# Strassen's seven products for five pairs of output tiles of a hybrid decoder layer, one Trainium2 core

## The chip, the core and the metric

The kernel runs on one core of one Trainium2 chip. The metric is the device time of one execution in microseconds (us): the median of several executions, lower is better. The core has TensorE (PE, the matrix unit), VectorE (DVE), ScalarE (ACT), GpSimd (POOL), and SyncE (SP), which here only issues DMA transfers. The engines run side by side, each through its own list of instructions in order, and wait for one another with semaphores.

## The reference

One layer of a decoder for 512 prompt tokens and 8 sample tokens, all in float32, d_model 2048.

```python
h = rms_norm(xp, norm_g[l])
u, gp, q, k, v, ga = split_proj(h, w_in[l])          # 2048 -> 6144
pm, pbuf = pool_mix(u, zero_buf, 0, pool_w[l], pool_scale[l])
a = dilated_attn_prompt(q, k, v, slopes)
xp = xp + merge_out(pm, gp, a, ga, w_out[l], xp.dtype)
...
y_prompt = rms_norm(xp, final_norm_g)
...
def merge_out(pm, gp, a, ga, w_out, dtype):
    mix = jnp.concatenate([pm * jax.nn.silu(gp), a * jax.nn.silu(ga)], axis=-1)
    return jnp.einsum('btm,md->btd', mix, w_out)     # 2048 x 2048: the part that changes
```

The same is done for the 8 sample tokens, which attend to a cache.

## The kernel before

**Layout.** Tokens lie along the free dimension: 520 columns (512 prompt, 8 sample), of which a matmul takes about half (260, or 256 and 264), since a PSUM bank holds 512 values. Features lie on the 128 partitions, 16 blocks of 128. Every float32 product is made of three matmuls: both operands are split into a high part, which is the value rounded to the matmul's input type, and the rest, the low part, and high times high, high times low and low times high are added up in PSUM. The moving side is in `mov_hi` and `mov_lo`. The weights come by DMA into `w_raw`, ACT writes the high part (`split_hi`, L884) and DVE the low part (`split_lo`, L1224).

**Stages.** The program is a list of steps. Steps 0 to 143 are the input projection in 144 chunks, 18 to a pair of heads, with the attention and the pooling branch of the previous and the present pair of heads woven in. Steps n = 0 to 47 after them (n counts from IN_CHUNKS = 144) are the output projection: 16 tiles of 128 output features, three chunks each (6, 5 and 5 of the 16 blocks of the contraction: 36, 30 and 30 matmuls). Tiles 0, 1 and 2 run interleaved (n = 0 to 8), since parts of the moving side still come in then. Tiles 3 to 13 follow one after another from n = 9, 96 matmuls each. Tiles 14 and 15 are done apart, first for the last 256 prompt tokens and the 8 samples (`half_chunk`, L719, n = 42 to 47), then for the first 256 tokens with the roles of weights and tokens exchanged (`row_chunk`, L730).

**What happens around a tile.** Each engine goes through the same list of steps. SP loads the chunk of step n + 3 (`load_chunk`, L452 to L459; it first waits until the slot of `w_raw` has been split). ACT and DVE split the chunk of step n + 2. One step after a tile's last chunk DVE transposes its 520 columns out of PSUM in blocks of 32 (`turn_out`, L1667 to L1669). Two steps after it SP sends the blocks to DRAM with 8 transfers (`send_tile`, L522 and L524), four steps after it SP reads them back in natural order with 2 transfers (`load_rows`, L530 and L532), five steps after it DVE adds the residual (`add_res`, L1682 and L1684), and ACT squares and sums the five row groups for the final norm (`y_square`, L1079). Six steps after it DVE multiplies with the final gain (`scale_y`, L1693 and L1694). SP loads the residual of a tile with 3 transfers (`load_res`, L537 to L540); those of tiles 0 to 2 are issued at n = 7, behind waits for the moving side to be split and for the k and v stores. `half_evict(14)` (L1068), at n = 45 on ACT, takes tile 14 out of PSUM, `turn_half(14)` (L737) on PE waits for it, and PE goes on with tile 15 behind it. After the last tiles a chain of small DVE and ACT instructions makes the norm and SP stores the rows.

**Queues.** No instruction of an engine passes another. SP's list holds the weight loads, `send_tile`, `load_rows` and `load_res` in the order of the steps. POOL has nothing to compute after the first 20 us of the program but issues some stores.

## Time and profile before

| what | value |
|---|---|
| median of 3 executions | 844.7 us (842.57 to 845.32) |
| span of the profiled execution, first to last instruction | 840.8 us |
| PE busy | 830.5 us, 99% of the span, 6825 matmuls |
| DVE busy | 566.8 us, 67% |
| ACT busy | 375.4 us, 45% |
| POOL busy | 60.8 us, 7% |
| DMA, mean over the span | 156 GB/s |
| output projection, tiles 3 to 13 on PE | 681.96 to 808.70 us |

The profiled execution has no total time of its own beside its span; the median of the three timed executions is 3.9 us above it, for what lies before the first and behind the last instruction. In the views below a name in the program such as `arena` stands for many buffers that share it. An instruction's duration reaches from its start to its result, so that consecutive instructions of one engine overlap in part: a matmul of 260 columns lasts about 280 ns, but a new one starts every 120 ns.

### The profile page before, as it was taken

What the parts mean: (1) busy time and instruction counts of PE and PEld (TensorE: products, weight loads), DVE (VectorE), ACT (ScalarE), POOL (GpSimd) and SP (SyncE); (2) the same over time, 40 slices, a digit from 0 to 9 for tenths busy, and PEclk for the clock granted to TensorE, in tenths of its full rate; (3) what the DMA queues carried; (4) which work ended last, traced back from release to release, by engine and by line L of the source; (5) the groups of instructions that cost most, each with busy time, mean ns of one, the idle gap of its engine ahead of it and who ended that gap; (6) DMA issues with size and microseconds to landing.
All of it is one profiled execution on the core that took longest, in us unless ns stands there. A gap on an engine that the chain in (4) does not pass through costs nothing.

```text
span 840.8 us, 17357 instructions
## 1 busy us (share of the span) xinstructions
PE 830.5 (99%) x6825; PEld 825.0 (98%) x6825; DVE 566.8 (67%) x1240; ACT 375.4 (45%) x821; POOL 60.8 (7%) x116
## 2 busy tenths in 40 slices
PE   9999999999999999999999999999999999999996
PEld 8999999999999999999999999999999999999995
DVE  5646784796579667957884797579888535444456
ACT  5745435523553454245535533553455325333444
POOL 2001100201010001001100201010000100000000
PEclk9999999999999999999999999999999999999998
DMA  8576247536643753575356437643768566766665
GB/s 291 149 174 166 84 126 181 134 96 171 165 115 87 192 148 82 150 183 145 92 134 170 128 94 201 166 111 93 179 184 279 162 168 172 179 178 176 177 169 204
DMA packets 274601, 131.51 MB, mean 156 GB/s; under 512 B 69056, under 2 KB 268160, under 8 KB 274496
## 3 DMA queue, kind: packets, MB, share of 16 engines
q1 hardware_dynamic: 269912, 122.90, 54.9%
q0 software_dynamic: 4608, 7.50, 2.7%
q8 instruction: 54, 0.88, 0.5%
q14 instruction: 27, 0.22, 0.1%
HBM read 110.32 MB, written 18.92 MB: 154 GB/s over the span
## 4 chain that ended last, share of the span: by engine, by line
PE 89%; DVE 4%; SPq 2%; DMA 2%; ACT 1%; issue 1%; DVEq 0%; ACTq 0%
PE pj L693 77%; PE ps_t L737 2%; PE ps_o L781 1%; PE ps_s L752 1%; PE ps_s L750 1%; PE ps_o L779 1%; DMA out<-arena 1%; SPq L486 1%; PE ps_o L693 1%; PE ps_s L798 1%; PE ps_t L798 1%; PE ps_s L693 1%; PE ps_s L631 1%; DVE w_lo L1224 1%; DVE arena L1339 1%
## 5 line engine op out<-in xcount | busy, mean ns | idle before, releaser
L693 PE MATMUL pj<-mov_hi,w_hi 128*128 128x260 f32 (+2 forms) x1952 | 399.2, 286 | 0.3 <-DVE mov_lo L1245 0.3
L693 PE MATMUL pj<-mov_hi,w_lo 128*128 128x260 f32 (+2 forms) x1952 | 392.9, 283 | 0.0
L693 PE MATMUL pj<-mov_lo,w_hi 128*128 128x260 f32 (+2 forms) x1952 | 392.4, 283 | 0.0
L693 PEld LDWEIGHTS pj<-mov_hi,w_hi 128*128 128x128 f32 x1952 | 300.9, 188 | 0.9 <-issue 0.7
L693 PEld LDWEIGHTS pj<-mov_hi,w_lo 128*128 128x128 f32 x1952 | 301.0, 188 | 0.0
L693 PEld LDWEIGHTS pj<-mov_lo,w_hi 128*128 128x128 f32 x1952 | 300.9, 188 | 0.0
L884 ACT ACTIVATE w_hi<-w_raw 128x640 fp32r<-128x640 f32 (+1 forms) x187 | 144.5, 773 | 261.4 <-PE pj L693 234.9
L1224 DVE TENSOR_TENSOR w_lo<-w_raw,w_hi 128x640 fp32r<-128x640 f32 (+1 forms) x187 | 161.7, 865 | 143.0 <-ACT w_hi L884 142.7
L944 ACT ACTIVATE pt_hi<-ps_t 128x128 fp32r<-128x128 f32 (+1 forms) x64 | 26.2, 436 | 80.3 <-PE ps_t L737 78.3
L1315 DVE TENSOR_TENSOR pt_lo<-ps_t,pt_hi 128x128 fp32r<-128x128 f32 (+1 forms) x64 | 29.7, 484 | 45.6 <-ACT pt_hi L944 45.4
L1262 DVE SCALAR_TENSOR_TENSOR arena<-pj,rstd_bc 128x260 f32<-128x260 f32 (+2 forms) x104 | 36.8, 398 | 12.1 <-PE pj L693 10.4
L928 ACT ACTIVATE arena<-arena,stat 128x128 f32<-128x128 f32 (+1 forms) x64 | 35.8, 559 | 19.3 <-DVE stat L1301 18.7
L1301 DVE CUSTOM_DVE_ANT_0 arena<-ps_s,arena 128x128 f32<-128x128 f32 (+1 forms) x64 | 29.7, 481 | 16.9 <-PE ps_s L752 16.9
L936 ACT ACTIVATE arena<-arena,stat 128x128 f32<-128x128 f32 (+1 forms) x64 | 34.2, 557 | 15.3 <-DVE stat L1309 15.2
L1079 ACT ACTIVATE arena<-arena 128x128 f32<-128x128 f32 (+1 forms) x70 | 21.7, 311 | 28.3 <-DVE arena L1684 26.6
L1375 DVE TENSOR_TENSOR arena<-arena 128x128 f32<-128x128 f32 (+3 forms) x48 | 28.8, 601 | 1.6
L1339 DVE TENSOR_TENSOR arena<-arena 128x1024 f32<-128x1024 f32 (+2 forms) x24 | 26.0, 1083 | 1.6 <-DMA out<-arena 1.6
L1342 DVE TENSOR_REDUCE arena<-arena 128x16 f32<-128x1024 f32 (+2 forms) x24 | 26.1, 1086 | 0.8
L737 PE MATMUL ps_t<-tab,arena 128*128 128x128 f32 x162 | 25.7, 273 | 0.6 <-DVE pt_lo L1315 0.5
L1366 DVE TENSOR_TENSOR arena<-arena 128x1024 f32<-128x1024 f32 (+2 forms) x24 | 25.4, 1086 | 0.2
L1183 POOL DMA_DIRECT2D out<-arena x32 | 16.3, 510 | 105.0 <-DVE arena L1614 105.0
L737 PEld LDWEIGHTS ps_t<-tab,arena 128*128 128x128 f32 x162 | 19.5, 141 | 3.1 <-ACT arena L936 0.7
(245 smaller groups left out, 810.5 us busy)
## 6 DMA issues: line engine op xcount, KB each, us to landing
w_raw<-in_w_in SPq DMA_DIRECT2D x96, 320.0 KB, 3.5
w_raw<-in_w_in SPq DMA_DIRECT2D x48, 384.0 KB, 3.7
arena<-in_cache_k_win SPq DMA_DIRECT2D x16, 384.0 KB
arena<-in_cache_v_win SPq DMA_DIRECT2D x16, 384.0 KB
w_raw<-in_w_out SPq DMA_DIRECT2D x16, 384.0 KB, 3.7
w_raw<-in_w_out SPq DMA_DIRECT2D x16, 320.0 KB, 3.9
arena<-in_cache_k_win SPq DMA_DIRECT2D x8, 512.0 KB
arena<-in_cache_v_win SPq DMA_DIRECT2D x8, 512.0 KB
```

The costliest lines, as they stand in the source:

```text
L693: mm = pe.matmul(dst[h][:, 0:own.stop - own.start], w, m[:, k, own], start=(k == 0 and i == 0), stop=(c == 2 and k == KT - 1 and i == 2))
L737: return pe.transpose(dst, src, ident[0:n, 0:n])
L884: act.activation(w_at(n)[0][:, 0:hi - lo, :], w_raw[:, n % SLOTS, 0:hi - lo, :], ACT.Copy).then_inc(w_hi_done, 1)
L928: act.activation(pb_, pb_, ACT.Exp, scale=-1.0, bias=nmax[:, i:i + 1], accum_out=den[:, i:i + 1]).then_inc(exped, 1)
L936: a = act.activation(pb_, pb_, ACT.Copy, scale=rden[:, i:i + 1])
L944: a = act.activation(pt_hi[:, 0:i + 1, P * i:P * i + P], ps_t[:, at:at + P * (i + 1)].rearrange("p (j x) -> p j x", j=i + 1), ACT.Copy)
L1224: dve.tensor_tensor(to_lo[:, 0:hi - lo, :], w_raw[:, n % SLOTS, 0:hi - lo, :], to_hi[:, 0:hi - lo, :].bitcast(F32), ALU.subtract).then_inc ...
L1262: o = dve.scalar_tensor_tensor(out=dst, in0=pj[a][h][:, c0:c1], scalar=scale, in1=rstd_bc[:, HT * h + c0:HT * h + c1], op0=ALU.mult, op1=A ...
L1301: dve.tensor_tensor_reduce(out=pbuf[r % 2][:, at:at + n], in0=ps_s[:, at:at + n], in1=nbias[:, SEQ - n:SEQ], scale=1.0, scalar=3e38, op0=A ...
L1315: o = dve.tensor_tensor(pt_lo[blk], ps_t[:, at:at + P * (i + 1)].rearrange("p (j x) -> p j x", j=i + 1), pt_hi[blk].bitcast(F32), ALU.subt ...
L1339: dve.tensor_tensor(ks, ks, q_rep.unsqueeze(1).to_broadcast([P, hi - lo, P]), ALU.mult).then_inc(kq_prod, 1)
L1375: o = dve.tensor_tensor(out, vv[:, P * to:P * (to + n)], vv[:, P * other:P * (other + n)], ALU.add)
```

## The change

Output tiles 3 to 12 are done as five pairs (m1, m2). The contraction of a pair is cut: blocks 0 to 3 and 4 to 7 of the moving side form a two by two problem with the two tiles and the two halves of the columns (260 each). It is done with seven block products in place of eight (Strassen's scheme in Winograd's form); blocks 8 to 15 are multiplied as before. A block product is 12 matmuls (4 blocks of the contraction, three matmuls each).

- **Weights.** A pair has eleven units of 4 blocks (512 columns): `w11`, `w12`, `w22`, the sums `s1` to `s4`, and `std1x`, `std1y`, `std2x`, `std2y` for the plain half. Each is split by ACT and DVE into a ring of six places (`unit_hi_of`, `unit_lo_of`). The four sums are made by POOL (`weight_sum`), in the order s1, s2, s3, s4, from the raw weights of 4 blocks each (`raw_a`, `raw_b`, `raw_c`, `raw_e`). s2 waits until s1 is split, since both use `raw_s`, and s4 until s2 is.
- **Moving side.** Once, at n = 2 to 7, DVE adds high and low parts of blocks 0 to 7 back together (`whole_x`, 2 instructions of 2080 columns), makes four combinations (`form_sums`, 4 of 1040 columns), and ACT and DVE split them (4 each of 1040 columns).
- **PSUM.** A pair uses four banks, a to d. The running sum in bank a is copied out by ACT at four points (`snapshot`), and PE waits for the copy before it goes on in that bank. `meet` (DVE) adds the snapshots to the banks, `turn_both` transposes a tile.
- **Steps.** A pair takes six steps k = 0 to 5 with 36, 24, 24, 36, 24 and 36 matmuls (`duo_step`), 180 in place of 192; in the first pair step k = 0 has only 12, since nothing is left over from a pair before. Pair 0 begins at n = 9, and tile 13 follows at n = 39 to 41 as a tile alone. The first tile of a pair is done in k = 4 and the second in k = 1 of the next pair.
- **SP.** A pair has 14 weight transfers where two tiles had 8. The residuals of tiles 0 to 2 are loaded at n = 8 and wait for the first two forms to be split (`m_split` 8).

Some semaphores are shared by two uses (`x_in`, `ms_done`, `sd_done`, `rs_done`), and several buffers lie over one another (`parts`); that is left out of the diff. In it, `...` marks what is left out.

```diff
+WOVEN = 3
+DUOS = 5
+SEVEN = WOVEN * 3
+DUO_STEPS = 6
+AFTER = SEVEN + DUOS * DUO_STEPS
+SOLO = WOVEN + 2 * DUOS
...
+RING = 6
+UNITS_OF = ("w11", "s1", "s2", "std1x", "std1y", "s3", "w12", "s4", "w22", "std2x")
+RING_SEQ = tuple((p - (u == "std2y"), u) for p in range(DUOS) for u in (
+    UNITS_OF[:1] + ("std2y",) * (p > 0) + UNITS_OF[1:])) + ((DUOS - 1, "std2y"),)
+RING_N = {pu: n for n, pu in enumerate(RING_SEQ)}
...
+        def chunk_at(step):
+            if IN_CHUNKS + SEVEN <= step < IN_CHUNKS + AFTER:
+                return None
+            return step if step < IN_CHUNKS + SEVEN else step - DUOS * DUO_STEPS
+        def duo_at(step):
+            n = step - IN_CHUNKS - SEVEN
+            return divmod(n, DUO_STEPS) if 0 <= n < DUOS * DUO_STEPS + 3 else None
+        def split_ahead(step):
+            n = step - IN_CHUNKS
+            if n <= SEVEN - 3 or n >= AFTER + 1:
+                return (chunk_at(step + 2),) if n < OUT_CHUNKS - 2 else ()
+            return {AFTER - 1: (chunk_at(step + 1),),
+                    AFTER: (chunk_at(step + 1), chunk_at(step + 2))}.get(n, ())
+        def units_ahead(step):
+            n = step - IN_CHUNKS - SEVEN
+            p, k = divmod(n, DUO_STEPS)
+            at = {0: ("s2", "std1x"), 1: ("std1y", "s3"), 2: ("w12", "s4", "w22"), 3: ("std2x",),
+                  4: ("std2y", "w11"), 5: ("s1",)}[k]
+            own = [(p + (u in ("w11", "s1")), u) for u in at]
+            own.sort(key=lambda pu: RING_N.get(pu, 0))
+            return [pu for pu in own if pu in RING_N]
...
+        def done_at(d):
+            if d < WOVEN:
+                return IN_CHUNKS + OUT_N[d, 2]
+            if d >= SOLO:
+                return IN_CHUNKS + 3 * d + 2
+            p, second = divmod(d - WOVEN, 2)
+            return IN_CHUNKS + SEVEN + DUO_STEPS * p + (7 if second else 4)
...
+            for step in range(STEPS):
+                if step + 3 < IN_CHUNKS + SEVEN:
                     load_chunk(step + 3)
+                elif step == IN_CHUNKS + AFTER - 2:
+                    load_chunk(IN_CHUNKS + SEVEN)
+                elif step == IN_CHUNKS + AFTER - 1:
+                    load_chunk(IN_CHUNKS + SEVEN + 1)
+                    load_chunk(IN_CHUNKS + SEVEN + 2)
+                elif step == IN_CHUNKS + AFTER:
+                    load_chunk(IN_CHUNKS + SEVEN + 3)
+                elif IN_CHUNKS + AFTER < step < STEPS - 3:
+                    load_chunk(chunk_at(step + 3))
+                if duo_at(step) and duo_at(step)[0] < DUOS:
+                    q, k = duo_at(step)
+                    for what, pair in {0: (), 1: (("a", 1), ("std2x", 0)),
+                                       2: (("b", 1), ("std2y", 0)), 3: (("c", 1), ("e", 1)),
+                                       4: (("std1x", 1),), 5: (("std1y", 1),)}[k]:
+                        if q + pair < DUOS:
+                            load_duo(q + pair, what)
                 for pr, j, p in due(step):
...
                 if n == 7:
+                    load_duo(0, "e")
+                    load_duo(0, "std1x")
+                    load_duo(0, "std1y")
+                if n == 8:
+                    sp.wait_ge(m_split, len(SPLIT_ORDER) + 2)
                     sp.wait_ge(m_split, len(SPLIT_ORDER))
...
-                        if step == last_chunk(e) + 2:
+                        if step == done_at(e) + 2:
                             send_tile(e)
-                        if step == last_chunk(e) + 4:
+                        if step == done_at(e) + 4:
+                            if e == 0:
+                                sp.wait_ge(m_split, len(SPLIT_ORDER) + 4)
...
+                    for e in range(3, KT):
+                        if step == done_at(e - 3) + 7:
+                            sp.wait_ge(y_scaled, e - 2)
+                            load_res(e)
...
+            def duo_step(p, k):
+                if k == 0:
+                    if p < DUOS:
+                        pe.wait_ge(*((yt_done, 1) if p == 0 else (met, 4 * p - 2)))
+                        unit(p, "w11", "a", [own_x(0, 0)], first="a")
+                    if p > 0:
+                        rest(p - 1, "std2y", "ad", last="ad")
+                if k == 1:
+                    pe.wait_ge(m_split, len(SPLIT_ORDER) + 4)
+                    if p > 0:
+                        pe.wait_ge(met, 4 * p - 1)
+                    unit(p, "s1", "c", [form_x("nt1")], first="c")
+                    pe.wait_ge(link_out, 4 * p + 1)
+                    unit(p, "s2", "a", [form_x("nt2")])
+                if k == 2:
+                    pe.wait_ge(*((yt_done, 2) if p == 0 else (c21_out, p)))
+                    pe.wait_ge(link_out, 4 * p + 2)
+                    rest(p, "std1x", "bc", first="b")
+                if k == 3:
+                    rest(p, "std1y", "bc")
+                    pe.wait_ge(link_out, 4 * p + 3)
+                    unit(p, "s3", "a", [form_x("t3")])
+                if k == 4:
+                    unit(p, "w12", "b", [own_x(KQ, 0)], last="b")
+                    unit(p, "s4", "c", [own_x(KQ, 1)], last="c")
+                if k == 5:
+                    pe.wait_ge(link_out, 4 * p + 4)
+                    unit(p, "w22", "a", [form_x("t4")])
+                    if p > 0:
+                        pe.wait_ge(met, 4 * p)
+                    rest(p, "std2x", "ad", first="d")
...
+            def snapshot(p, u):
+                i = ("w11", "s1", "s2", "s3").index(u)
+                act.wait_ge(unit_used, RING_N[p, u] + 1)
+                if p > 0:
+                    act.wait_ge(met, 4 * p - (2, 3, 1, 0)[i])
+                elif u == "s3":
+                    act.wait_ge(own_done, PAIRS)
+                bank = duo_banks(p)["c" if u == "s1" else "a"]
+                act.activation(snap[u], bank[:, 0:HT], ACT.Copy).then_inc(link_out, 1)
+            def take_c21(p):
+                act.wait_ge(unit_used, RING_N[p, "std2y"] + 1)
+                act.wait_ge(yt_done, WOVEN + 2 * p + 1)
+                act.activation(both[:, 0:HT], duo_banks(p)["a"][:, 0:HT],
+                               ACT.Copy).then_inc(c21_out, 1)
+            def duo_early(p, k):
+                if k == 1 and p > 0:
+                    take_c21(p - 1)
+                if k == 2 and p < DUOS:
+                    snapshot(p, "s2")
+                if k == 4 and p < DUOS:
+                    snapshot(p, "s3")
+            def duo_late(p, k):
+                if k == 0 and p < DUOS:
+                    snapshot(p, "w11")
+                if k == 1 and p < DUOS:
+                    snapshot(p, "s1")
...
                 for d in range(KT - 2):
-                    if step == last_chunk(d) + 5:
+                    if step == done_at(d) + 5:
                         y_square(d)
-                if step == TAIL + 3:
+                if step == IN_CHUNKS + 3 * (KT - 2) + 3:
                     half_evict(KT - 2)
...
+            def weight_sum(p, u):
+                to, one, other = {"s1": (raw_s, raw_b, raw_c), "s2": (raw_s, raw_s, raw_a),
+                                  "s3": (raw_b, raw_b, raw_a), "s4": (raw_s, raw_s, raw_e)}[u]
+                if u == "s3":
+                    pool.wait_ge(unit_sum, 4 * p + 2)
+                elif (p, u) == (0, "s1"):
+                    pool.wait_ge(w_lo_done, IN_CHUNKS + SEVEN)
+                else:
+                    before = {"s1": (p - 1, "s4"), "s2": (p, "s1"), "s4": (p, "s2")}[u]
+                    pool.wait_ge(unit_lo, RING_N[before] + 1)
+                if u == "s1":
+                    pool.wait_ge(b_in, X_IN + 16 * (p + 1))
+                    pool.wait_ge(c_in, X_IN + 32 * (p + 1))
+                elif u == "s4":
+                    pool.wait_ge(e_in, X_IN + 32 * (p + 1))
+                else:
+                    pool.wait_ge(a_in, X_IN + 16 * (p + 1))
+                pool.tensor_tensor(to, one, other, ALU.add).then_inc(unit_sum, 1)
+            for p in range(DUOS):
+                for u in ("s1", "s2", "s3", "s4"):
+                    weight_sum(p, u)
...
+            def meet(p, out, bank, s, last):
+                if last is not None:
+                    dve.wait_ge(unit_used, RING_N[p, last] + 1)
+                dve.wait_ge(link_out, 4 * p + 4)
+                dve.tensor_tensor(out, bank[:, 0:HT] if last else bank, snap[s],
+                                  ALU.add).then_inc(met, 1)
+            def turn_both(d):
+                to = y_sq[d % 3]
+                dve.wait_ge(y_st[d % 3], Y_ST * (d // 3))
+                dve.transpose(to[:, 0:SEQ], both[:, 0:SEQ])
+                dve.transpose(to[:, SEQ:SEQ + SQ].rearrange("p (a b) -> p a b", b=NB),
+                              both[:, SEQ:NT].unsqueeze(1).to_broadcast(
+                                  [P, SQ // NB, NB])).then_inc(yt_done, 1)
+            def duo_out(p, k):
+                if k == 1 and p > 0:
+                    dve.wait_ge(c21_out, p)
+                    meet(p - 1, both[:, HT:NT], duo_banks(p - 1)["d"], "s3", "std2y")
+                if k == 2 and p > 0:
+                    dve.wait_ge(met, 4 * p)
+                    dve.wait_ge(c21_out, p)
+                    turn_both(WOVEN + 2 * p - 1)
+                if k == 5 and p < DUOS:
+                    banks = duo_banks(p)
+                    meet(p, snap["s3"], snap["s1"], "s3", None)
+                    meet(p, both[:, 0:HT], banks["b"], "w11", "w12")
+                    meet(p, both[:, HT:NT], banks["c"], "s2", "s4")
+                    dve.wait_ge(met, 4 * p + 3)
+                    turn_both(WOVEN + 2 * p)
...
+                if n in (2, 3):
+                    whole_x(n - 2)
+                if n in (4, 5):
+                    form_sums(n - 4)
+                if n == 6:
+                    form_lo_of("nt1")
+                    form_lo_of("t3")
+                if n == 7:
+                    form_lo_of("nt2")
+                    form_lo_of("t4")
```

## Rows read from the trace of the kernel before

**Rows 1.** The page: busy time and share of each engine.

```profile
PE 830.5 (99%) x6825; PEld 825.0 (98%) x6825; DVE 566.8 (67%) x1240; ACT 375.4 (45%) x821; POOL 60.8 (7%) x116
```

**Rows 2.** Chain that ended last, 640 to 841 us: start, length (us), what.

```profile
681.96 126.74 PE pj L693 x1056
...
816.29 0.38 ACT arena L1068
...
817.26 3.64 PE pj L719 x30
820.90 2.14 PE pj L730 x18
```

**Rows 3.** Who waited for whom, 640 to 841 us: in total, times, longest (us).

```profile
PEld ps_t L737 <- ACT arena L1068: 0.3, 1, 0.3
```

**Rows 4.** Windows: stretch, length, busy PE, PEld, DVE, ACT, POOL, clock, DMA share, GB/s.

```profile
751.00:774.00 23.00, 23.00 (x194) 23.00 (x193) 9.92 (x21) 8.45 (x26) 0.00 (x0) 1.00 0.68 177
```

**Rows 5.** Single tiles: ns min/median/max, first and last start; 512 columns.

```profile
L1031 ACT ACTIVATE pw_hi<-arena x4: 632/632/633, 104.7 to 576.7; 128x512 fp32r<-128x512 f32 x4
L1597 DVE TENSOR_TENSOR pw_lo<-arena,pw_hi x4: 683/684/684, 107.1 to 579.2; 128x512 fp32r<-128x512 f32 x4
```

**Rows 6.** Groups of instructions, shapes apart: xcount, busy us, mean ns; POOL's sum.

```profile
L1154 POOL TENSOR_TENSOR arena<-arena 128x512 f32<-128x512 f32 x1 | 1.0, 1042 | 3.2 <-DMA arena<-in_x_prompt 3.2
```

**Rows 7.** The page's groups: DVE on 1024 columns.

```profile
L1339 DVE TENSOR_TENSOR arena<-arena 128x1024 f32<-128x1024 f32 (+2 forms) x24 | 26.0, 1083 | 1.6 <-DMA out<-arena 1.6
```

**Rows 8.** Window from the first added DVE work to step n = 9.

```profile
661.30:681.90 20.60, 20.60 (x174) 20.60 (x173) 8.72 (x17) 6.54 (x10) 0.00 (x0) 1.00 0.56 142
```

**Rows 9.** Timeline of SP's queue: first residual load, read back of tiles 0 and 1.

```profile
669.77 0.47 SPq L537 DMA_DIRECT2D arena<-in_x_prompt  x1
...
685.08 0.95 SPq L530 DMA_DIRECT2D arena<-y_scratch  x1
...
690.69 0.49 SPq L530 DMA_DIRECT2D arena<-y_scratch  x1
```

**Rows 10.** Timeline of ACT: squares of tiles 0 and 1, and the split between.

```profile
692.40 0.31 ACT L1079 ACTIVATE arena<-arena 128x128 f32<-128x128 f32 x1 [1.69 <-DVE arena L1684]
...
694.45 0.72 ACT L884 ACTIVATE w_hi<-w_raw 128x640 fp32r<-128x640 f32 x1
...
696.86 0.31 ACT L1079 ACTIVATE arena<-arena 128x128 f32<-128x128 f32 x1 [1.68 <-DVE arena L1684]
```

**Rows 11.** DMA issues, 681 to 808 us: count, KB each, median us to landing.

```profile
w_raw<-in_w_out SPq DMA_DIRECT2D x12, 384.0 KB, 3.8
...
w_raw<-in_w_out SPq DMA_DIRECT2D x11, 192.0 KB, 2.6
```

**Rows 12.** Timeline of SP's queue, tile 13: send, last weight load, read back.

```profile
809.63 0.34 SPq L522 DMA_DIRECT2D y_scratch<-arena  x1
...
812.81 0.83 SPq L452 DMA_DIRECT2D w_raw<-in_w_out  x2
813.88 0.38 SPq L530 DMA_DIRECT2D arena<-y_scratch  x1
```

**Rows 13.** Windows behind the last matmul; the clock is the third figure from the end.

```profile
835.00:836.00 1.00, 0.00 (x0) 0.00 (x0) 0.86 (x6) 0.37 (x1) 0.00 (x0) 0.77 1.03 397
836.00:837.00 1.00, 0.00 (x0) 0.00 (x0) 1.00 (x4) 0.75 (x2) 0.00 (x0) 0.50 0.75 293
```

**Rows 14.** Timeline of PE: soon after the start, and its last matmul.

```profile
8.24 1.78 PE L631 MATMUL ps_s<-mov_lo 128*128 128x260 f32 x8
...
832.32 0.28 PE L730 MATMUL pj<-pooled_lo,mov_hi 128*128 128x256 f32 x1
```

**Rows 15.** Timelines of POOL and DVE at 10 us: two instructions that overlap.

```profile
10.23 0.61 POOL L1154 TENSOR_TENSOR arena<-arena 128x256 f32<-128x256 f32 x1 [0.80 <-DMA arena<-in_x_prompt]
10.30 1.10 DVE L1252 TENSOR_TENSOR w_lo<-w_raw,w_hi 128x512 fp32r<-128x512 f32 x1
```

338 lines of the change are left out of this document (278 added, 60 removed).

## The prediction, made before the changed kernel was run

> **What bounds the kernel now.** I read the page's busy shares first: PE is at 99%, the others at 67% and less [rows 1]. The chain that ended last is then followed through the stage that changes. It is one piece there, 1056 matmuls (tiles 3 to 13) in 126.74 us without a gap, so 120.0 ns for a matmul [rows 2]. The windows say the same: PE busy 23.00 of 23.00 us at full clock, DVE 9.9, ACT 8.5, POOL 0 [rows 4]. So each matmul taken out is worth 0.120 us, as long as PE never waits. Behind it PE waits once, for 0.3 us, for ACT's copy of tile 14 (L1068) [rows 3], and from there the chain goes on over tile 15 (L719), 18 matmuls of L730 and the chain of the last norm [rows 2]. Whatever delays that copy delays the end. The question is therefore which of the new waits are covered, and I follow the queues that feed them with the durations of the rows.
>
> **The matmuls taken out.** A pair has 180 for 192, five pairs save 60: 60 x 0.120 = **-7.2 us**. Runs of matmuls into one bank cost nothing extra: L719 does that and takes 3.64 / 30 = 121 ns for 264 columns [rows 2]. The 14 more waits of PE in a pair cost nothing where they are already met, as now at each chunk.
>
> **The added splits and sums.** A split of 512 columns takes 0.63 us on ACT and 0.68 on DVE [rows 5], so a pair has 11 x 0.63 = 7.0 and 11 x 0.68 = 7.5 us. With snapshots of 0.38 (as L1068) [rows 2], squares, meets, transposes and residuals I get 13 us for ACT and 15 for DVE of the pair's 21.6 us. POOL's sum of 512 columns takes 1.04 us, four make 4.2 [rows 6]. SP has 14 weight transfers, and 13 for each of two tiles, at about 0.4 us each (a tile's eight sends take 3.1 us, 809.63 to 812.81 [rows 12]): 16 of 21.6 us. No engine becomes the bound. In pairs 1 to 4 I find each handover met: bank a's last snapshot is asked for one step after PE is done with s3. I take 0 for them, and for the range 0 to 0.7 a pair.
>
> A DVE split and a POOL sum do get in each other's way: at 10.30 us a 512-column split lasted 1.10 us in place of 0.68, beside a POOL instruction that had begun at 10.23 [rows 5, 15]. The Trainium skill, page "SBUF — State Buffer", section "Who interferes with whom", says that a DVE instruction with two SBUF inputs and a GpSimd instruction that reads SBUF shut each other out for a whole instruction. By it twenty sums could hold DVE for up to 20 x 1.04 = 21 us in all; DVE has the room, so the sum would change only in the start of pair 0.
>
> **Start of pair 0 (n = 2 to 9).** Added on DVE: 2 x 2.2 us (2080 columns) and 8 x 1.1 (1040 columns), by 1083 ns for 1024 [rows 7], 13.2 us. Its idle time between 661.3 and 681.9 was 20.6 - 8.7 = 11.9 [rows 8]. So the low part of s1 is ready near 683.3, in time for PE, which starts w11 at 681.96 and takes 1.44 us for a unit. s2 comes after POOL 1.04, ACT 0.63 and DVE 0.68, near 685.8, and PE wants it at 684.8. I take **+1.0** (0.2 to 1.6).
>
> **First pair, fourth snapshot.** PE's step k = 5 needs the snapshot after s3. In ACT's list it stands behind the squares of tiles 0 and 1 (n = 11 and 12), which wait for a round trip through DRAM. Now SP's list: the residual loads of tiles 0 to 2 were issued from 669.77 [rows 9]; now they wait for two forms to be split, near 677.0. Nine transfers to 680.8, two sends to 687.0, three weight transfers to 688.4, tile 0's read back to 689.4, tile 2's send to 692.5, three weight transfers, and tile 1's read back is issued at 693.9 instead of 690.69 [rows 9]. It lands after 3.0 us (256 KB, between 2.6 for 192 KB and 3.8 for 384 [rows 11]), DVE adds 0.9, and the squares begin at 697.8 and not 696.86. They take 2.1 us (692.40 to 694.45) [rows 10], the snapshot 0.38: 700.3. PE asks for it at 682.0 + 1.0 + 120 matmuls (14.4) = 697.4. **+3.0**. Even with the old times of tile 1 the snapshot would end at 696.9 + 2.1 + 0.4 = 699.4, +2.0; landing 1 us later makes it +4.
>
> **From pair 0 to pair 1.** w11 of pair 1 waits for the second meet of pair 0, which in DVE's list is behind s1 of pair 1. After the snapshot ACT does two splits (1.1), DVE splits the second (0.7) and adds tile 2's residual (0.9), ACT squares tile 2 (2.2) and splits s1 (0.6), DVE splits it (0.7) and does two meets (0.8): 7.0 us. PE has 36 matmuls meanwhile, 4.3 us. **+2.7** (0 if tile 2's part were out of the way). From pair 1 on the squares stand at k = 0 and 3, not between these.
>
> **The tail.** Tile 12 is now the second of a pair and is done at n = 40 where it was 38, and its transpose stands on DVE behind the split of chunk n = 43, whose ACT half waits for PE's chunk n = 40. Let T be the end of that chunk (681.96 + 1026 x 0.120 = 805.0 before [rows 2]). Split 0.84 and 0.96, transpose 0.9: T + 2.9. SP: send tile 12 to 6.0, two loads to 7.0, send tile 13 to 10.1, two loads to 11.0; before, only tile 13's send was in that place, from 809.63, and its read back was issued at 813.88, T + 8.9 [rows 12]. Tile 12's read back goes at T + 11.0, lands at 14.1, is added by 15.4, squared by 17.5, and only then, since `y_square(12)` falls on n = 45 ahead of `half_evict(14)`, tile 14 is copied: T + 17.9. Before, the copy was at 816.29, T + 11.3 [rows 2], with no squares ahead of it. PE arrives at T + 3.6 + 66 x 0.121 = T + 11.6: it waits 6.3 us, 0.3 before. **+6.0** (5 to 7.5 with landings of 2.6 to 3.8 us and a little more).
>
> **The clock.** After its last matmul, at 832.32 us [rows 14], PE idled and its granted clock fell to 0.50, 1.2 GHz, at about 835.5 (0.77 in the window from 835) [rows 13], some 3 us after. The tail's wait is longer than that. At the lower level 260 columns took (1.78 - 0.28) / 7 = 0.214 us [rows 14] and not 0.120. Between `turn_half(14)` and the next chain are 48 matmuls [rows 2]: 0 to 48 x 0.094 = 4.5 us, as the level comes back at once or not in them. I take the lower middle, **+2.0**. In pair 0 such a loss would fall into the 2.7 us that PE waits anyway.
>
> **Sum.** -7.2 + 1.0 + 3.0 + 2.7 + 6.0 + 2.0 = +7.5 us: a span of 848.3 for 840.8. The profiled execution's span is 3.9 us below the median of the timed ones, 844.7; I carry that over: **852.2 us**.
>
> **The rivals.**
> - *Faster, the handovers are covered.* Speaks for it that all engines but PE are half idle [rows 4]. Needed: tiles 0 to 2 and tile 12 come back from DRAM before their squares are ACT's next work. Then -7.2 + 1.0 leaves 838.5; with a rest of 3 us in the tail 841.5. Against it stands SP's list, whose issue times are read and not guessed. 0.22.
> - *About the same, one of the two places only.* If the tail holds PE by 5 to 6 us but pair 0 doesn't, or the other way round, and the clock stays up, -7.2 + 1.0 + 6.0 gives 844.5. 0.16.
> - *Slower, as forecast*, from both places: 847.5 to 856. 0.52.
> - *Slower in each pair.* Transfers are cut smaller and land later, and by the stand-off of DVE and POOL the splits come later; when they are 1.5 us or more late, the round trip of a pair's first tile holds up the fourth snapshot in every pair as it does in the first. Four times 0.7 to 1.5 on top of the forecast, and 1 us more at each of the three places: 858 to 861. 0.10.
> - That the products are not saved can't be: the steps' matmuls can be counted in the code.
>
> **How the numbers follow.** The likeliest case is the forecast, 852.2. The range runs from 839, the covered case with a small rest, to 859, the forecast with late landings and the full clock loss; some 0.1 lies on each side. A change of 0.3% (2.5 us) is about what a measurement of this kernel can tell from none: faster 0.22, within 0.16, slower 0.52 + 0.10 = 0.62.
>
> **What would show it.** Right: 6765 matmuls; PE idle before the unit w22 of pair 0 (released by ACT's snapshot), before w11 of pair 1 (by DVE's meet) and before `turn_half(14)` (by ACT's copy, right behind squares of tile 12), about 3, 2.7 and 6.3 us; a granted clock under 1.00 after the last. The read back of tile 12 issued some 11 us after the end of chunk n = 40. Wrong: squares of tiles 0, 1 or 12 that start well before these times, or PE gapless from 682 us on; then the queue on SP is shorter than I count. Gaps of equal size in all five pairs would speak for the last rival.

## The result, and the profile after the change

| | kernel before | changed kernel |
|---|---|---|
| median of the runs (lowest to highest) | 845.0 us (842.6 to 845.4, 4 runs) | 861.6 us (860.7 to 862.8, 4 runs) |
| span of the profiled execution | 840.8 us | 858.9 us |
| matmuls | 6825 | 6765 |
| from the first matmul of tile 3 (unit w11 of pair 0) to the end | 159.0 us | 177.2 us |

The changed kernel is slower: ratio 1.0207, 95% interval 1.0188 to 1.0225. The forecast was 852.2 us, from 839 to 859; the time is outside. The direction was right, the size was not: +7.5 us were forecast and +16.6 measured.

Up to tile 3 the two kernels run alike: w11 of pair 0 starts at 681.63 us, tile 3 of the kernel before at 681.79. (The 681.96 of [rows 2] is where that piece of the chain begins, 0.17 us behind the first matmul of tile 3.) All of the difference is behind that. The page of the changed kernel, busy times first, then two lines of the 40 slices:

```profile
span 858.9 us, 17511 instructions
PE 829.5 (97%) x6765; PEld 822.4 (96%) x6765; DVE 604.7 (70%) x1285; ACT 394.7 (46%) x875; POOL 90.1 (10%) x136
PE   9999999999999999999999999999999969999965
PEclk9999999999999999999999999999999989999988
```

PE is busy for 1.0 us less than before [rows 1] with 60 matmuls less: the saving of 7.2 us is there, and more than half of it went into matmuls at a lower clock (4.1 us, below). Some of the rest is in how busy time is counted, about 0.16 us at each idle stretch (below). The longer span is idle time. Who waited for whom from 640 us on, PE's rows (total, times, longest, us):

```profile
PE pj L1030 <- ACT tab L1374: 6.6, 1, 6.6
PE ps_t L916 <- ACT arena L1322: 6.5, 1, 6.5
PE pj L1030 <- issue: 3.3, 3, 1.6
PE pj L1030 <- DVE w_lo L2105: 1.8, 2, 1.6
```

The kernel before had 0.3 us there [rows 3]. The same waits in PE's timeline (start, length, what, and in brackets the idle time before it and its releaser):

```profile
683.45 0.48 PE L1030 MATMUL pj<-parts,w_hi 128*128 128x260 f32 x2 [0.21 <-DVE w_lo L2105]
686.71 0.48 PE L1030 MATMUL pj<-parts,w_hi 128*128 128x260 f32 x2 [1.59 <-DVE w_lo L2105]
705.00 0.80 PE L1030 MATMUL pj<-parts,w_hi 128*128 128x260 f32 x2 [6.56 <-ACT tab L1374]
742.29 0.36 PE L1030 MATMUL pj<-mov_hi,w_hi 128*128 128x260 f32 x1 [1.21 <-issue]
765.81 0.36 PE L1030 MATMUL pj<-mov_hi,parts 128*128 128x260 f32 x1 [1.56 <-issue]
788.15 0.36 PE L1030 MATMUL pj<-mov_hi,parts 128*128 128x260 f32 x1 [0.56 <-issue]
831.67 0.69 PE L916 MATMUL ps_t<-tab,arena 128*128 128x128 f32 x2 [6.52 <-ACT arena L1322]
```

These are, in order: units s1 and s2 of pair 0; w22 of pair 0; the first rest unit (std1x) of pairs 2, 3 and 4; the turn of tile 14's half. A row counts the idle time from the modelled end of the matmul before it. I take it from start to start less one 0.12 us matmul, which gives 0.16 more: 2.1 us at the start of pair 0, 6.7 in pair 0, 4.1 in the later pairs (with 0.3 before w22 of pair 1), 6.7 at the tail.

The clock, in windows of PE (stretch, length, busy, granted clock, DMA share, GB/s):

```profile
696.00:702.00 6.00, 2.44 (x21) 1.00 0.75 207
703.00:709.00 6.00, 4.00 (x18) 0.50 0.54 155
710.00:716.00 6.00, 5.95 (x50) 1.00 0.37 81
824.00:829.00 5.00, 1.15 (x10) 1.00 0.64 181
830.00:835.00 5.00, 3.33 (x15) 0.50 0.22 63
836.00:840.00 4.00, 4.00 (x35) 1.00 0.00 0
```

PE stood from 698.3 to 705.0 us and from 825.0 to 831.7. Within each of these stretches its granted clock fell from 1.00 to 0.50 (2.4 to 1.2 GHz) and came back some 7 us later; the matmuls meanwhile started 0.216 us apart in place of 0.120. That is 22 x 0.096 = 2.1 us in pair 0. At the tail the two turns of halves start 8.1 us apart where they were 6.2: 2.0 us.

Why w22 waited: ACT's timeline in pair 0. L1333 are squares, L1374 is the fourth snapshot.

```profile
696.40 0.31 ACT L1333 ACTIVATE arena<-arena 128x128 f32<-128x128 f32 x1 [6.02 <-DVE arena L2042]
702.55 0.31 ACT L1333 ACTIVATE arena<-arena 128x128 f32<-128x128 f32 x1 [3.49 <-DVE arena L2042]
704.59 0.36 ACT L1374 ACTIVATE tab<-pj 128x260 f32<-128x260 f32 x1
```

The order is the one forecast, the time is not: the squares of tile 1 start 5.7 us later than before [rows 10]. At the tail both are as forecast. The read back of tile 12 on SP, and on ACT the first of its squares and behind them the half eviction of tile 14 (L1322):

```profile
824.85 0.50 SPq L641 DMA_DIRECT2D arena<-y_scratch  x1
829.21 0.31 ACT L1333 ACTIVATE arena<-arena 128x128 f32<-128x128 f32 x1 [1.55 <-DVE arena L2042]
831.25 0.36 ACT L1322 ACTIVATE arena<-pj 128x264 f32<-128x264 f32 x1
```

Back in pair 0, SP's queue: first residual load, first send, read back of tile 0, of tile 1.

```profile
678.94 0.38 SPq L648 DMA_DIRECT2D arena<-in_x_prompt  x1
682.82 0.43 SPq L633 DMA_DIRECT2D y_scratch<-arena  x1
691.35 0.38 SPq L641 DMA_DIRECT2D arena<-y_scratch  x1
697.29 0.49 SPq L641 DMA_DIRECT2D arena<-y_scratch  x1
```

In the kernel before these read backs went at 685.08 and 690.69 [rows 9]. SP issues with hardly a pause from 678.9 to 702 us. What stands at the head of its list waits for the forms' low parts, and those ran beside GpSimd's first sum. Timelines of POOL and of DVE, there and in pair 1; POOL's second row is a sum with no DVE instruction beside it:

```profile
675.60 2.21 POOL L1553 TENSOR_TENSOR w_raw<-tab,extra 128x512 f32<-128x512 f32 x1 [17.52 <-DVE w_lo L1580]
726.95 1.29 POOL L1553 TENSOR_TENSOR w_raw<-tab,extra 128x512 f32<-128x512 f32 x1 [9.98 <-DMA extra<-in_w_out]
736.03 1.67 POOL L1553 TENSOR_TENSOR w_raw<-w_raw 128x512 f32<-128x512 f32 x1 [0.63 <-DVE parts L2105]
```

```profile
675.43 3.48 DVE L2092 TENSOR_TENSOR parts<-arena,parts 128x1040 fp32r<-128x1040 f32 x2
736.48 1.77 DVE L2039 TENSOR_TENSOR arena<-arena 128x512 f32<-128x512 f32 x1
```

Alone, such a DVE operation takes 0.69 us on 512 columns, and POOL's sum of 512 columns took 1.04 in the kernel before [rows 6]; here all 20 took 1.26 to 2.21. Not all of that comes from the two running side by side, as the sum at 726.95 shows: it took 1.29 alone. And what 736.48 delayed, in ACT's timeline: squares of tile 4, the eviction of C21 (L1380), two splits and the snapshot that std1x waits for.

```profile
738.48 0.31 ACT L1333 ACTIVATE arena<-arena 128x128 f32<-128x128 f32 x1 [2.71 <-DVE arena L2042]
740.53 0.36 ACT L1380 ACTIVATE arena<-pj 128x260 f32<-128x260 f32 x1
741.83 0.36 ACT L1374 ACTIVATE rstd_bc<-pj 128x260 f32<-128x260 f32 x1
```

### The profile page after: what moved, and what is told of

Read it like the earlier page. It is cut to its first block, busy times and chain, and to the rows that moved or that the text cites. A ratio compares the mean times of both kernels' runs of the same rounds, so it can differ in the third digit from the quotient of the medians.

```text
span 858.9 us, 17511 instructions
## 1 busy us (share of the span) xinstructions
PE 829.5 (97%) x6765; PEld 822.4 (96%) x6765; DVE 604.7 (70%) x1285; ACT 394.7 (46%) x875; POOL 90.1 (10%) x136
## 4 chain that ended last, share of the span: by engine, by line
PE 80%; DVE 5%; issue 4%; DMA 3%; SPq 3%; ACT 3%; POOL 1%; DVEq 0%; ACTq 0%; POOLq 0%
PE pj L872 63%; PE pj L1030 5%; PE ps_t L916 2%; PE ps_o L960 1%; PE ps_s L931 1%; PE ps_s L929 1%; PE ps_o L958 1%; POOL w_raw L1553 1%; ACT arena L1333 1%; DMA extra<-in_w_out 1%; DMA out<-arena 1%; DVE w_lo L2105 1%; SPq L657 1%; PE ps_s L977 1%; PE ps_t L977 1%
## 5 line engine op out<-in xcount | busy, mean ns | idle before, releaser
L872 PE MATMUL pj<-mov_hi,w_hi 128*128 128x260 f32 (+1 forms) x1600 | 328.6, 287 | 0.3 <-DVE mov_lo L1601 0.3
L872 PE MATMUL pj<-mov_hi,w_lo 128*128 128x260 f32 (+1 forms) x1600 | 322.1, 283 | 0.0
L872 PE MATMUL pj<-mov_lo,w_hi 128*128 128x260 f32 (+1 forms) x1600 | 321.3, 282 | 0.0
L872 PEld LDWEIGHTS pj<-mov_hi,w_hi 128*128 128x128 f32 x1600 | 246.4, 189 | 0.9 <-issue 0.6
L872 PEld LDWEIGHTS pj<-mov_hi,w_lo 128*128 128x128 f32 x1600 | 246.4, 188 | 0.0
L872 PEld LDWEIGHTS pj<-mov_lo,w_hi 128*128 128x128 f32 x1600 | 246.4, 188 | 0.0
L1671 DVE TENSOR_TENSOR parts<-ps_t,parts 128x128 fp32r<-128x128 f32 (+1 forms) x64 | 29.7, 485 | 44.9 <-ACT parts L1198 44.8
L1618 DVE SCALAR_TENSOR_TENSOR arena<-pj,rstd_bc 128x260 f32<-128x260 f32 (+2 forms) x104 | 37.0, 400 | 12.1 <-PE pj L872 10.3
L1030 PE MATMUL pj<-mov_hi,w_hi 128*128 128x260 f32 x144 | 41.3, 287 | 1.3 <-issue 1.2
L1030 PE MATMUL pj<-mov_lo,w_hi 128*128 128x260 f32 x144 | 41.1, 285 | 0.0
L1030 PE MATMUL pj<-mov_hi,w_lo 128*128 128x260 f32 x144 | 41.0, 285 | 0.0
L1333 ACT ACTIVATE arena<-arena 128x128 f32<-128x128 f32 (+1 forms) x70 | 21.7, 310 | 38.0 <-DVE arena L2042 36.2
```

The lines of the kernel that those rows point to most:

```text
L872: mm = pe.matmul(dst[h][:, 0:own.stop - own.start], w, m[:, k, own], start=(k == 0 and i == 0), stop=(c == 2 and k == KT - 1 and i == 2))
L1030: mm = pe.matmul(dst, w[:, own], m(k), start=(at in first and k == 0 and i == 0), stop=(at in last and k == KQ - 1 and i == 2), skip_group ...
L1333: act.activation(sq_junk[0:n, :], src, ACT.Square, accum_out=ss_y[0:n, t, d:d + 1]).then_inc(y_squared, 1)
L1618: o = dve.scalar_tensor_tensor(out=dst, in0=pj[a][h][:, c0:c1], scalar=scale, in1=rstd_bc[:, HT * h + c0:HT * h + c1], op0=ALU.mult, op1=A ...
L1671: o = dve.tensor_tensor(pt_lo[blk], ps_t[:, at:at + P * (i + 1)].rearrange("p (j x) -> p j x", j=i + 1), pt_hi[blk].bitcast(F32), ALU.subt ...
```

## The experiments

My theory after the trace: PE waits where an ACT or DVE instruction that it needs stands in its engine's list behind one for an older tile, which waits for a round trip through DRAM. The rivals: GpSimd and DVE holding each other up; SP's queue as the real cause; the clock.

The table has all runs. Columns 2 to 6 are PE's idle time in us by place in the profiled execution (start of pair 0; before w22 of pair 0; before w11 of pair 1; elsewhere in pairs 1 to 4; tail), column 7 the time from the end of the last matmul to the end, column 8 from w11 of pair 0 to the end. Up to w11 single executions differ by up to 3 us, so column 8 compares traces best. The ratio (95% interval) compares times: each is to the kernel before as it was timed again beside that version (medians 842.9 to 843.5 us), not to the 845.0 of the first row.

| kernel | start | w22 | w11 | pairs | tail | rest | from w11 | median us | ratio to before |
|---|---|---|---|---|---|---|---|---|---|
| before | - | - | - | 0 | 0.2 | 8.2 | 159.0 | 845.0 | 1 |
| changed | 2.1 | 6.7 | 0.2 | 4.1 | 6.7 | 9.3 | 177.2 | 861.6 | 1.0207 (1.0188-1.0225) |
| e1_tail | 2.1 | 6.8 | 0.2 | 3.8 | 2.8 | 10.7 | 172.5 | 857.1 | 1.0166 (1.0144-1.0188) |
| e5_tail_first | 2.1 | 6.7 | 0 | 3.2 | 3.2 | 10.5 | 171.8 | 858.0 | 1.0174 (1.0151-1.0197) |
| e2_pair0 | 2.1 | 0.1 | 4.6 | 2.4 | 6.8 | 10.0 | 173.7 | 858.1 | 1.0167 (1.0147-1.0186) |
| e6_pair0_all | 2.1 | 1.1 | 3.6 | 5.0 | 7.3 | 9.7 | 175.9 | 859.3 | 1.0193 (1.0178-1.0208) |
| e7_res_queue | 3.4 | 1.1 | 2.3 | 1.5 | 6.7 | 9.3 | 173.3 | 858.5 | 1.0179 (1.0155-1.0204) |
| e4_steady | 2.2 | 6.2 | 0.9 | 0.2 | 9.0 | 9.1 | 174.8 | 858.7 | 1.0175 (1.0153-1.0196) |
| e3_fill | 0 | 7.9 | 0.6 | 0 | 6.9 | 9.7 | 172.3 | 856.9 | 1.0159 (1.0136-1.0183) |
| e11_fill3 | 1.0 | 6.9 | 0 | 0 | 6.5 | 10.0 | 172.0 | 857.2 | 1.0160 (1.0143-1.0176) |
| e14_sums_dve | 1.2 | 6.9 | 1.1 | 2.1 | 7.4 | 9.1 | 176.8 | 861.0 | 1.0212 (1.0195-1.0229) |
| e8_all | 2.2 | 0.5 | 3.8 | 0 | 5.2 | 10.6 | 168.6 | 852.3 | 1.0104 (1.0087-1.0121) |
| e9_fixed | 2.1 | 0 | 4.2 | 0.4 | 2.6 | 10.5 | 164.9 | 850.0 | 1.0077 (1.0064-1.0089) |
| e10_fixed_dve | 1.2 | 0 | 4.0 | 0.3 | 2.5 | 9.7 | 165.1 | 849.0 | 1.0067 (1.0053-1.0080) |
| e12_meets_first | 2.2 | 0 | 2.3 | 2.1 | 2.8 | 10.3 | 163.4 | 847.4 | 1.0045 (1.0028-1.0061) |
| e13_meets_dve_ev | 1.2 | 0 | 3.3 | 0.2 | 0 | 12.5 | 162.0 | 846.5 | 1.0035 (1.0025-1.0046) |
| e15_weights_early | 1.2 | 0 | 0.9 | 5.0 | 0 | 12.8 | 163.7 | 848.2 | 1.0057 (1.0043-1.0071) |
| e16_own_residual | 1.1 | 0 | 1.9 | 4.1 | 1.9 | 11.7 | 166.2 | 850.2 | 1.0074 (1.0059-1.0090) |
| e17_pair0_weights | 1.1 | 0 | 1.8 | 1.5 | 0 | 12.2 | 160.1 | 844.8 | 1.0023 (1.0012-1.0033) |
| e18_residual_late | 1.2 | 0 | 1.7 | 1.3 | 1.2 | 11.1 | 160.3 | 844.0 | 1.0001 (0.9991-1.0011) |

What matmuls at the lower clock cost is in column 8 alone: nothing in e12, e15, e17 and e18, about 1.5 us in e9, e13 and e16, about 2 in e1, e5 and e8, 3 to 5 in the others.

The expectations count "from the first unit" from unit s1, 1.4 to 1.9 us behind w11; the 158.6 us that one of them gives for e13 was counted from s2 by mistake and is 160.6 from s1.

**The tail, e1 and e5.** In ACT's loop the half eviction moves up, in e1 ahead of the squares, in e5 ahead of the split too:

```diff
+                if step == IN_CHUNKS + 3 * (KT - 2) + 3:
+                    half_evict(KT - 2)
                 for d in range(KT - 2):
                     if step == done_at(d) + 5:
                         y_square(d)
-                if step == IN_CHUNKS + 3 * (KT - 2) + 3:
-                    half_evict(KT - 2)
```

> One line is moved: ScalarE takes the half eviction of tile 14 before the five squares of tile 12, at the same step; nothing else changes. Theory (a place in ScalarE's order): the 6.5 us that TensorE waits for L1322 near the end are 5 squares and the read back that they wait for, and the slow matmuls at clock 0.5 behind them are a consequence of that idle stretch. Then the wait falls to 0.3 us as in the kernel before (6.4 us), the clock stays at full speed between 829 and 836 (2.0 us), and the span falls by 7.5 to 9 us, to 850-851.4. Rival (the eviction is late in itself, because the chunk's splits and the turn of tile 12 are late on both engines): the wait falls by 0 to 3 us only, and the span stays above 855. Rival on the clock (the drop belongs to the matmuls' form in the tail and not to the wait): 6.4 us are won and the slow stretch stays, span 852.5.

The wait fell from 6.7 to 2.8 us, not to 0.3. The clock stayed at 1.00 behind the shorter wait. ACT's timeline of e1 shows what else stood ahead of the eviction:

```profile
827.70 0.63 ACT L1138 ACTIVATE parts<-w_raw 128x512 fp32r<-128x512 f32 x1 [3.10 <-DMA w_raw<-in_w_out]
828.24 0.37 ACT L1322 ACTIVATE arena<-pj 128x264 f32<-128x264 f32 x1
```

> ScalarE takes the half eviction of tile 14 ahead of the high split of chunk 47 as well as ahead of the squares of tile 12; nothing else changes. In e1 the eviction still stood behind that split, whose weights landed 3.1 us after the chunk before them, because SyncE issued them behind the eight transfers that send tile 13. Theory (two things stood ahead of the eviction, each late by SyncE's queue): the wait of TensorE, 6.7 us in the changed kernel and 2.8 in e1, is under 0.5 us; counted from the first unit of pair 0 to the end (175.4 us in the changed kernel, 170.7 in e1) this kernel takes 167.5-169 us; span 852-854. Rival (the last matmuls wait for the late chunk 47 anyway, and the wait only moves behind the next chunk): 170-171 us from the first unit, span within 1 us of e1.

The rival held. Turning tile 14's half cost nothing now, but PE waited 1.1 us for the weights of chunk 47 and 2.1 us for tile 15's half eviction, behind the squares of tile 13. From s1 to the end it took 170.0 us, e1 170.7. The order on ACT and the late weights give one wait, and taking away the first shows the second.

**Pair 0, e2, e6 and e7.** e2 and e6 place tiles 0 to 2 one step later (`later(d)` is 1 for d < 3, otherwise 0), e6 the adds too:

```diff
-                    if step == done_at(d) + 5:
+                    if step == done_at(d) + 5 + later(d):
                         y_square(d)
...
-                    if step == done_at(d) + 6:
+                    if step == done_at(d) + 6 + later(d):
                         scale_y(d)
```

> The squares, scaling and next residual loads of tiles 0, 1 and 2 are each placed one step later, so that the fourth snapshot of pair 0 stands ahead of the squares of tile 1 on ScalarE. Theory (order): the 6.7 us before the w22 unit of pair 0 and the 2.1 us of slow matmuls behind them go; the squares still wait for their tiles but nothing of TensorE's waits for them; span 849.5 to 851. Rival (late transfers: SyncE's queue started the residual loads 2 us late and each tile lands late, so the wait only moves to the next thing that stands behind the squares, the splits of pair 1's first weights): 2 to 5 us of the 6.7 come back in pair 1, span 853 to 857. Third: the squares of tile 1 now sit ahead of the high half of s1 of pair 1, which is due 1.4 us later than the snapshot was late, then about 3 us stay.

> Adds, squares, scaling and next residual loads of tiles 0, 1 and 2 are each placed one step later, so that VectorE too meets pair 0's half products ahead of the add of tile 2. In e2 (squares alone) 4.6 us of TensorE's wait came back before w11 of pair 1, behind VectorE's adds of tiles 1 and 2, whose tiles landed at 701.6 and 705. Theory (queue order on both engines, behind tiles that land late): both waits go, and with them the slow matmuls; from the first unit of pair 0 to the end 166.5-169 us (changed kernel 175.4, e2 172.0); span 850-852.5. Rival (the tiles' late landing is what counts and something third stands behind it: the sum of s1 of pair 1 or a residual load): 170-172 us.

The wait before w22 went, and 4.6 us of it came back before w11 of pair 1. DVE's timeline of e2: the adds of tiles 1 and 2 wait for their read backs, the meet stands behind them.

```profile
701.77 0.69 DVE L2042 TENSOR_TENSOR arena<-arena 128x512 f32<-128x512 f32 x1 [4.35 <-DMA arena<-ys_scratch]
705.27 0.69 DVE L2042 TENSOR_TENSOR arena<-arena 128x512 f32<-128x512 f32 x1 [1.42 <-DMA arena<-ys_scratch]
708.17 0.41 DVE L2116 TENSOR_TENSOR arena<-pj,extra 128x260 f32<-128x260 f32 x1
```

e6 missed both expectations: moving the adds as well left 1.1 and 3.6 us, and from s1 it took 174.1 us. e7 leaves all places and issues the nine residual loads of tiles 0 to 2 from GpSimd's queue:

```diff
                     weight_sum(p, u)
+                    if (p, u) == (0, "s1"):
+                        for d in range(3):
+                            pool.dma_start(x_res[d][:, 0:SEQ]...
+                            ...
```

> The nine residual loads of tiles 0 to 2 are issued by GpSimd between its first two sums in place of SyncE; every place on ScalarE and VectorE stays as changed. SyncE's nine issues took 3.9 us (678.9 to 682.8) ahead of the first send of a tile. Theory (SyncE's queue sets when tiles 0 and 1 land, and the wait of 6.7 us is that landing): the sends begin at 680.5 in place of 682.8 and the second tile lands about 2 us earlier, TensorE's wait before w22 of pair 0 falls to 4-5.2 us, and from the first unit of pair 0 to the end it takes 173-174 us (175.4). Rival (landings are set by the quarter loads and by the steps, not by these nine): the wait stays at 6.2-6.8 us. A risk: GpSimd's nine issues of some 0.5 us run into the sum of s2 (start of pair 0 up to 1 us later).

The squares of tile 1 began at 700.33 us (702.55), as SP's queue predicts, and the wait before w22 was 1.1 us in place of 6.7. Only half of those 5.6 us is the queue's doing: counted from w11, w22 started 2.8 us sooner (20.6 for 23.4). The other half is that PE came later. The named risk came true: the nine issues delayed the sum of s2, the start of pair 0 cost 3.4 us, and behind it the granted clock was 0.50 from 689.6 to 692.8 us. From w11 to the end 4.0 us were won, but 2.6 of them in the gaps of the later pairs, where nothing had been moved; why isn't shown. So SP's queue is a cause of the wait in pair 0, and the places on ACT and DVE decide who pays for it.

**GpSimd, e3, e11 and e14.** In e3 and e11 the sums are left out, their tiles are filled:

```diff
-                pool.tensor_tensor(to, one, other, ALU.add).then_inc(unit_sum, 1)
+                pool.memset(to, 0.01).then_inc(unit_sum, 1)
```

> GpSimd writes a constant over the sum's tile in place of adding two tiles, under the same waits: it reads no SBUF (the weight sums are left out, so four of ten products are of a constant). Theory (order on ScalarE makes the large waits, the stand-off of GpSimd and VectorE the small ones): VectorE's two-input operations beside GpSimd go back from 1.2-1.8 us to 0.7-1.1, the gaps of 1.75, 1.36, 1.73 and 0.72 us at the start of pair 0 and before the first rest unit of pairs 2 to 4 shrink by 3 to 5 us together, and the waits of 6.7 us in pair 0 and at the tail stay within 1 us; span 854 to 856. Rival (the stand-off also makes pair 0's wait, by holding back the form's low parts and with them the residual loads): that wait falls by 2 us or more, span 851 to 853. Rival (GpSimd costs nothing): span within 1 us of 858.9.

> The changed kernel with each GpSimd sum replaced by three fills of its tile one after the other, 3 x 0.53 us and the waits between them, about as long as the sums' 1.3-2.2 us, but with no read of SBUF (the weight sums are left out). In e3 one fill took the sum's place, and 5 us went with it: 0.53 us is shorter than a sum, and nothing stood off VectorE. Theory (stand-off: what costs is VectorE held back by GpSimd's reads): VectorE's operations stay at 0.69 us as in e3 and at most 1 us of the 5.2 comes back; span 853-855. Rival (the length of the sum in the chain sum, high half, low half, matmul is what costs): the gaps at the start of pair 0 (0.4 and 1.75 us) come back by 1 us or more, and in pairs 2 to 4 by 1.5-3 us together; span 856-859.

The start and the gaps of pairs 2 to 4 went: 5.0 us from w11 to the end. The two large waits stayed. Yet the rival has a part in pair 0: the first residual load went at 677.59 us in place of 678.94, and counted from w11 the squares of tile 1 and w22 started 1.1 us sooner. PE came 2.3 us sooner, so its wait grew all the same. With three fills of 1.7 us in all, longer than most sums, they stayed away too, except 1.0 us at the start. So it isn't the sum's length but its reading beside DVE. The adds of residuals, 675 to 792 us (count, busy us, mean ns), in the changed kernel, in e3 and in e11:

```profile
L2039 DVE TENSOR_TENSOR arena<-arena 128x512 f32<-128x512 f32 x9 | 9.5, 1051 | 10.1 <-DMA arena<-ys_scratch 10.1
```

```profile
L2039 DVE TENSOR_TENSOR arena<-arena 128x512 f32<-128x512 f32 x10 | 6.9, 690 | 12.1 <-DMA arena<-ys_scratch 12.1
```

```profile
L2043 DVE TENSOR_TENSOR arena<-arena 128x512 f32<-128x512 f32 x10 | 6.9, 690 | 9.5 <-DMA arena<-ys_scratch 9.5
```

> The changed kernel with its 20 weight sums on VectorE, as in e10, and nothing else moved. Theory (stand-off costs 4-5 us of the 16.6, all at the start of pair 0 and before the first rest unit of pairs 2 to 4; the large waits are places in ScalarE's queue): the start falls from 2.1 to 1-1.3 us, the gaps in pairs 2 to 4 from 3.8 us to under 1, the waits of 6.7 and 6.7 us stay within 1 us; span 853.5-856.5. Rival (VectorE is full in the steps of the squares, and 14 us of sums more make it late): the gaps in pairs 2 to 4 stay, span 857-860.

e14 makes the sums on DVE (`dve.tensor_tensor` in place of `pool.tensor_tensor`, each a step ahead of its high half). DVE's operations took 0.69 us again, and still the kernel was no faster: 2.1 us stayed in the pairs, 1.1 before w11, 7.4 at the tail. Most of what GpSimd cost, 20 sums cost on DVE. Of the two expectations the one with a full DVE is the nearer.

**The later pairs, e4, and all together, e8.** e4 has `later(d)` 1 for tiles 4, 6, 8 and 10; e8 joins e4, e5 and e6.

> The squares, scaling and next residual loads of the second tile of each pair (tiles 4, 6, 8 and 10) are placed one step later, behind the eviction of C21 of the pair that follows. Theory (the 1.36, 1.73 and 0.72 us before the first rest unit of pairs 2 to 4 come down the chain of 2 us of squares, then the eviction of C21, then the splits and the snapshot): these gaps go, span 855 to 856. Rival (they come from the sum and the splits of s2, late by landings and by GpSimd): they stay, span within 1 us of 858.9.

The gaps of the later pairs went from 4.1 to 0.2 us, as in e3: both GpSimd and the squares are links of one chain, and taking out either mends it. But the tail's wait rose to 9.0 us: counted from w11, PE got there 4.8 us sooner and the eviction let it go on only 2.5 us sooner (147.5 us for 150.0). From w11 to the end 2.5 us were kept.

> The moves of e5, e6 and e4 together: eviction of tile 14 first; adds, squares, scaling and residual loads of tiles 0 to 2 one step later; squares, scaling and residual loads of tiles 4, 6, 8 and 10 one step later. Theory (the time lost was waits behind an engine's own queue, 60 matmuls fewer are really worth 7.2 us): only the 2.1 us at the start of pair 0 stay, no slow stretch in the pairs or before the last rows; span 837.5-841 and time 841-845, a ratio to the kernel before of 0.996-1.000. Rival (behind each removed wait stands the next, because the tiles still land late): 2-4 us come back in pair 1 or before the last chunks, span 841-846, time 845-850.

The rival held, and more: 168.6 us from w11, with waits of 3.8 us in pair 0 and 5.2 at the tail. The trace named the next places. ACT had the high half of s1 of pair 1 behind the squares of tile 1. DVE had the transpose of tile 12 behind the low split of chunk 45:

```profile
808.14 0.96 DVE L1583 TENSOR_TENSOR w_lo<-w_raw,w_hi 128x768 fp32r<-128x768 f32 x1 [4.37 <-ACT w_hi L1141]
809.02 0.70 DVE L2123 STREAM_TRANSPOSE arena<-arena 128x512 f32<-128x512 f32 x1
```

**Mending the next places, e9, e10, e12 and e13.** e9: squares of tiles 0 to 2 two steps later, transpose of tile 12 ahead of that split, half eviction of tile 14 one step earlier. e10: e9 with the sums on DVE. e12: e9 with the meets of step 5 ahead of the low half of s1. e13: e12 with the sums on DVE and tile 15's half eviction ahead of tile 13's squares.

> e8 with three places moved further: squares, scaling and next residual loads of tiles 0 to 2 two steps later than in the changed kernel (in e8 the squares of tile 1 held the high half of s1 of pair 1, and that held VectorE and the meets behind it: 3.8 us); the turn of tile 12 ahead of the low split of chunk 45 on VectorE (in e8 it stood 4 us behind it, and with it the eight sends on SyncE and the weights of chunks 46 and 47 behind them: 1.6, 0.3, 1.2 and 2.1 us); the half eviction of tile 14 one step earlier. GpSimd still makes the sums. Theory (queue order and what queues behind it): only the 2.1 us at the start of pair 0 stay; span 837-841 where e8 had 850.5, time 841-845, ratio to the kernel before 0.995-1.001. Rival (tiles that land late): 2-5 us come back somewhere in pairs 1 and 2, span 841-845, ratio 1.000-1.006.

> e9 with the 20 weight sums on VectorE in place of GpSimd, each one step ahead of its high half (s1 at step 4, s2 at step 5, s3 at step 0, s4 at step 1 of a pair); nothing of GpSimd runs in the pairs. Theory (the stand-off of GpSimd and VectorE makes the start of pair 0 late, and each sum is 0.7 us on VectorE in place of 1.3-2.2 on GpSimd): VectorE's two-input operations all take 0.7 us, the 0.4 and 1.75 us at the start of pair 0 fall by 1.5-2.1, and nothing else is lost since VectorE has idle time; 1-2.5 us faster than e9, span 836-839. Rival (VectorE's queue is what is full: its own 20 x 0.7 = 14 us push the lows and the meets): 1-5 us slower than e9.

> e9 with one more place moved: at step 5 of a pair VectorE meets the half products ahead of the low half of s1 of the next pair (in e9 that low half waited until 705.6 for its high half, for the sum on GpSimd and for the quarter of weights behind them, issued at 698.6 on SyncE behind eight sends and a read back). Theory (a place in a queue): the 4.2 us before w11 of pair 1 and the slow matmuls behind them (1 us) go; left are 2.1 us at the start of pair 0 and 2.6 us at the tail; span 840.5-843, time 842.5-845.5, ratio to the kernel before 0.998-1.003. Rival (late landing: w11 starts on time and the unit of s1 behind it waits instead): 2.5-4 us of the 4.2 come back before the s1 unit of pair 1; span 844-846.5, ratio 1.003-1.006.

> e12 with the sums on VectorE in place of GpSimd (as e10) and the half eviction of tile 15 ahead of the squares of tile 13 (in e9 TensorE waited 1.9 us for it). Theory: another 1-1.5 us at the start of pair 0 and 1-1.9 us at the tail are won on e12, span 838-841, ratio 0.995-1.001. Rival (the tail is bound by the squares and the residual load of tile 15, which now come later by the eviction): nothing is won at the tail, span 840-842.5.

By column 8 each move of a place won, each less than the order alone would have it. In e9 the transpose went at 802.58 us and tail waits fell from 5.2 to 2.6, but 4.2 us stayed before w11 of pair 1. e10 is no faster than e9 by the trace (165.1 and 164.9), as e14 said. In e12 half of the 4.2 stayed, and pair 1 cost 2.1 us (0.4 in e9). In e13 PE no longer waited at the tail, and the time behind its last matmul rose from 10.3 to 12.5 us, so that e13's rival held there. What held the meets in e12, in ACT's timeline, is the second rest of weights:

```profile
701.53 0.64 ACT L1365 ACTIVATE parts<-w_raw 128x512 fp32r<-128x512 f32 x1 [4.41 <-DMA w_raw<-in_w_out]
```

**SP's queue and the last residual, e15 to e18.** e15 issues two of a pair's weight loads a step earlier on SP, ahead of sends. e17 does it in pair 0 alone:

```diff
                     loads = {0: (), 1: (("a", 1), ("std2x", 0)), ...
+                    if q == 0:
+                        loads[1] += (("std2y", 0),)
+                        loads[2] = (("b", 1), ("c", 1))
+                        loads[3] = (("e", 1),)
```

> e13 with two loads of quarter weights one step earlier on SyncE in each pair (the second rest of the y part, and the c quarter of the next pair), ahead of the sends and read backs that they stood behind. In e12 the weights of std2y of pair 0 were issued late and ScalarE took them 4.4 us after it was free; VectorE's low half, the add and the meets stood behind. Theory (SyncE's queue is what made the last 3.25 us): that wait falls under 1 us; the span from the first unit of pair 0 to the end falls by 2-3 us on e13's 158.6, to 155.6-156.8; time 843.5-845, ratio to the kernel before 1.000-1.003. Rival (each send delayed by the loads delays a tile in turn): the wait stays over 2.5 us or comes back within pair 1.

> e15 with the residual of tile 15 loaded into memory of its own (free after the last pair), so that it needn't wait until tile 12 has been squared and scaled; tile 12 is the second of its pair and is done 3 chunks later than in the kernel before. In e13 that load was issued at 823.6 (816.0 in the kernel before), landed at 827.4, and the last adds, norms and stores follow it. Theory: the add of tile 15 comes about 1.5 us earlier, at the turn's own time, and the stretch from the last matmul to the end falls from 12.7 to 11 us; 1-2 us on e15, time 842-843.5, ratio 0.998-1.001. Rival (squares and scaling of tiles 12 and 13 on VectorE and ScalarE bound the end by themselves): under 0.5 us.

e15's wait before w11 fell to 0.9 us, but pairs 1 to 3 now lost 1.4 to 1.7 us each, and it was slower than e13. ACT's and PE's timelines in pair 1 of e15: squares of the pair's first tile, then the fourth snapshot, then w22. This is the last rival of the prediction, at work.

```profile
721.14 0.31 ACT L1336 ACTIVATE arena<-arena 128x128 f32<-128x128 f32 x1 [5.37 <-DVE arena L2023]
723.19 0.36 ACT L1377 ACTIVATE tab<-pj 128x260 f32<-128x260 f32 x1
```

```profile
723.60 0.51 PE L1033 MATMUL pj<-parts,w_hi 128*128 128x260 f32 x2 [1.57 <-ACT tab L1377]
```

e16, e15 with tile 15's residual in memory of its own, put that load on SP ahead of the last two weight loads, and PE waited 1.9 us for those.

> e13 with the early loads of e15 in pair 0 alone; SyncE's order in pairs 1 to 4 and at the tail is e13's. Theory (SyncE's queue is full only beside the sends of tiles 0 to 2): the wait before w11 of pair 1 is 0.9 us as in e15 (3.25 in e13), the later pairs lose nothing, 1.5-2.5 us on e13: time 844-845, ratio to the kernel before 1.001-1.002. Rival (any issue moved ahead of a send comes back as a late tile): 1.4 us or more before w22 of pair 1, and the ratio stays 1.003 or more.

> e17 with the residual of tile 15 in memory of its own, issued right behind the read back of tile 13 (819 in place of 823.6) and behind all weights. Theory: half_add of tile 15 no longer waits 1.1 us for it, and the stretch from the last matmul to the end falls from 12.7 to 11.2-11.7 us: 1-1.5 us on e17, time 842.7-844, ratio 0.999-1.001. Rival (ScalarE's and VectorE's squares and scaling of tiles 12 and 13 bound the end): under 0.5 us.

e17 kept the pairs nearly whole (1.5 us, most of it before w22 of pair 1, so that part of its rival is true) and took 160.1 us from w11. The wait before w11 of pair 1 was 1.8 us, not the 0.9 of e15 that was expected. e18 issues the residual of tile 15 behind all weights, without waiting for tile 12 to be scaled. In e13 it had gone at 823.58 us, and DVE had waited for it:

```profile
827.50 0.42 DVE L2212 TENSOR_TENSOR arena<-ps_s,arena 128x256 f32<-128x256 f32 x1 [1.12 <-DMA arena<-in_final_norm_g]
```

In e18 this wait is gone and the rest is 11.1 us, but PE waited 1.2 us for the last weights, so that from w11 to the end its trace is no shorter than e17's; its median is 0.8 us lower. The kernel is level with the one before: 1.0001, interval 0.9991 to 1.0011. It doesn't beat it. From w11 e18 takes 160.3 us where the kernel before took 159.0: 7.2 us less of matmuls, 5.2 us more of waits (1.2 + 1.7 + 1.3 + 1.2, against 0.2), and a rest longer by 2.9, leave +0.9; about 0.3 us I can't assign.

## Why the prediction was wrong

The mechanism of the two large waits was right. What failed: the later pairs' handovers were taken as met, at 0 us, and cost 4.1; pair 0 was sized at 5.7 us with the clock's loss hidden in a wait, and cost 9.0; the start of pair 0 was sized at 1.0 and cost 2.1; and 1.1 us behind the last matmul weren't in the sum. The measured terms are differences of the two profiled executions. Their spans are 18.1 us apart and the medians 16.6, since the profiled execution of the kernel before is the fastest of its four.

| term | forecast | measured |
|---|---|---|
| 60 matmuls | -7.2 | -7.2 |
| start of pair 0 | +1.0 | +2.1 |
| pair 0, fourth snapshot, then meets of pair 1, with the clock | +3.0 + 2.7 | 6.7 + 0.2 + 2.1 = +9.0 |
| pairs 1 to 4 | 0 | +4.1 |
| tail | +6.0 | 6.7 - 0.2 = +6.5 |
| clock at the tail | +2.0 | +2.0 |
| behind the last matmul | 0 | 9.3 - 8.2 = +1.1 |
| sum | +7.5 | +17.6 of 18.2 from w11; 0.6 not assigned |

*The matmuls.* Right. 6765 of them, and 180 in a row took 0.120 us each in the later pairs.

*The start of pair 0.* The step that failed is the price of POOL and DVE side by side. [Rows 15] had shown 1.10 for 0.68 us, and the prediction took the sum at 1.04 and the forms' low parts at 1.1 each. Two of the latter took 3.48 us, the sum 2.21. The sum was also priced too low by itself: 1.29 us with nothing beside it. The Trainium skill, page "SBUF — State Buffer", section "Who interferes with whom", says that a DVE instruction with two SBUF inputs and a GpSimd instruction exclude each other for a whole instruction when the latter reads SBUF, and don't when it only writes. The traces agree with both: 0.69 against 1.77 us in the changed kernel, 0.69 throughout beside the fills of e11. I cited the rule and then let it change only this one place.

*Pair 0.* The mechanism was right, its size was not. The terms mis-sized: the residual loads began at 678.94 us for 677.0 (1.1 of it from the low parts just named, by e3); tile 0's read back went at 691.35 for 688.4, because weight and send issues queued longer; tile 1's at 697.29 for 693.9; its squares began 5.3 us behind it, for 3.9 (the landing took longer). So 702.55 for 697.8. The 2.7 us from pair 0 to pair 1 weren't a second wait beside the first, as the sum had it: they are the same late tiles, seen from DVE, and come out when the first is mended (e2: 4.6). And with 6.7 us of idle time the clock's loss did not hide in a wait.

*Pairs 1 to 4.* This step failed outright. Each handover was called met because both sides had room on average. The chain sum beside add, squares, C21, splits, snapshot has no room: 1.1 us more on the add (1.77 for 0.69) came through to PE as 0.7 to 1.7 us in pairs 2 to 4, and e3 and e4 each took that away from one end of the chain. The last rival, slower in each pair, had the stand-off and late landings in it, but through the first tile and the fourth snapshot; here it was the second tile and C21. Its time, 858 to 861, came nearest, with a chance of 0.10.

*The tail and its clock.* Right in mechanism and size: 6.5 for 6.0, 2.0 for 2.0. Chunk n = 40 ended at 813.4 us, so the read back of tile 12 went 11.4 us behind it (forecast 11.0), and the copy of tile 14 came 17.9 behind it (17.9). The 2.0 was the lower middle of a range from 0 to 4.5, so that this match is in part luck. The price of a slow matmul, 0.214 us, came from a row at 8.24 us for which the trace gives no lower clock; here, in windows at 0.50, 260 columns took 0.216 and 264 took 0.220. e1 and e5 add that the squares were the first of several things in line.

*Behind the last matmul.* Not in the sum, and its cause stays open. In both kernels the last DVE instruction ends 4.4 us behind the last matmul; the 1.1 us lie behind that, where the stores of the rows go out (4.9 us for 3.8). It is not the residual of tile 15, which reuses tile 12's memory and so is loaded later: in the changed kernel DVE's add of it waited for PE alone.

```profile
840.33 0.42 DVE L2203 TENSOR_TENSOR arena<-ps_s,arena 128x256 f32<-128x256 f32 x1 [5.05 <-PE ps_o L916]
```

That residual's wait shows only where PE no longer waits at the tail (e13, e17), and e18 takes it away.

*The range.* The upper ends of the prediction's own terms (1.6, 4, 2.7, 0.7 in each of four pairs, 7.5 and 4.5, less 7.2) add up to 860.6 us; it ended at 859. The start of pair 0, pair 0 and the later pairs came out above their upper ends. The median was taken to stand 3.9 us above the profiled span. In all later runs an execution's time stands 1.8 to 2.0 us above its own span, so the profiled execution of before was the one of 842.6 us, and 2.1 of the 3.9 were spread between runs. The changed kernel's median stands 2.7 us above its profiled span; the span was missed by 10.6 us (858.9 for 848.3), the median by 9.4.

## What to carry to other kernels

Saved matmuls are worth their full time, but only once every in-order list that feeds TensorE has room at the step where it's needed, and none of the eighteen versions here got below the kernel before. Price a chain link by link, not an engine by its mean load. Where two late things share one cause (here SyncE's full queue), don't add their waits, and expect that moving one instruction up only shows the next. Before adding GpSimd work that reads SBUF, list which two-input VectorE instructions fall beside it, and who waits for those.

## What was not expected of the hardware

- GpSimd's sum of 512 columns took 1.29 us with no VectorE instruction beside it (1.04 in the kernel before), and up to 2.21 beside VectorE; VectorE's add of the same size 1.77 us beside it, 0.69 alone; an add of 8x128 took 1.36 us beside a sum (e12), 0.27 alone. Beside fills of 0.53 us VectorE kept its 0.69.
- The granted clock fell within idle stretches of PE of 6.7 us and stayed at 0.50 for about 7 us, with matmuls running in it. In e1 (2.8 us idle) and e12 (2.3) it stayed at 1.00. In e13 (3.3 us idle), e10 (2.5, at the tail) and e16 (1.9, before w11 of pair 1) it fell to 0.50 for some 3 us, and only after PE had gone on (e16: PE went on at 705.11, and the window from 705.6 to 708.8 shows 0.50). The length of the last wait alone doesn't tell whether the clock falls.
- The read back of a tile (256 KB and 4 KB, two issues), with weights, sends and residuals in flight, had landed 4.1 us after its first issue in pair 0 (691.35 us, tile 0), where I had put 3.0.
